# A BF16 product on TensorE in place of VectorE's additions for the band mask of windowed attention, in one hybrid encoder block

## The reference

```python
sc = jnp.einsum('bnqhgd,bnkhd->bnhgqk', qb, kb).astype(jnp.float32) * (ATT_HD ** -0.5)
...
valid = (jnp.abs(qpos[:, :, None] - kpos[:, None, :]) <= WINDOW) \
    & (kpos >= 0)[:, None, :] & (kpos < s)[:, None, :]
sc = jnp.where(valid[None, :, None, None], sc, -jnp.inf)
m = jnp.maximum(jnp.max(sc, axis=-1, keepdims=True), snk)
p = jnp.exp(sc - m)
p = p / (jnp.sum(p, axis=-1, keepdims=True) + jnp.exp(snk - m))
```

## Time and profile before

| | |
|---|---|
| median of 3 runs | 1995.5 us (1993.83 to 1995.56) |
| the profiled execution, its own time | 1994.98 us |
| its span | 1993.2 us |
| PE busy | 98% of the span |
| DVE busy | 67% |
| ACT busy | 40% |
| mean granted TensorE clock | 0.995 of full speed |
| attention stage (1016 to 1182 us) | 166 us |

### The profile page before, as it was taken

One profiled execution on the slowest core, in us unless ns is written; L12 is line 12 of the kernel. 1 busy time (PEld: TensorE's weight loads), 2 busy tenths in 40 slices (PEclk: granted clock), 3 DMA queues, 4 the chain that ended last, 5 costly groups with the idle time before them and its releaser, 6 DMA issues. The chain is left out here.

```text
span 1993.2 us, 25435 instructions
## 1 busy us (share of the span) xinstructions
PE 1958.0 (98%) x8988; PEld 1600.0 (80%) x8988; DVE 1338.9 (67%) x1646; ACT 802.8 (40%) x1066; POOL 851.3 (43%) x569
## 2 busy tenths in 40 slices
PE   7999999999999999999999999999999999999997
PEld 5888888888888778888876678888888888878886
DVE  7866666677676855466876665457866666677666
ACT  6433333345554432222135453335333333355542
POOL 0344444368776222422222212242434334577782
PEclk9999999999999999999999999999999999999998
DMA  3333232356353142412111134341433332474532
GB/s 136 114 118 108 89 116 97 135 200 233 127 164 117 63 148 91 179 43 65 42 64 43 64 107 137 128 156 53 137 100 109 106 100 91 146 267 150 197 104 85
DMA packets 110331, 235.74 MB, mean 118 GB/s; under 512 B 9648, under 2 KB 30256, under 8 KB 110256
## 3 DMA queue, kind: packets, MB, share of 16 engines
q1 hardware_dynamic: 79424, 186.15, 27.5%
q10 hardware_dynamic: 30832, 48.60, 7.1%
HBM read 169.18 MB, written 65.54 MB: 118 GB/s over the span
## 5 line engine op out<-in xcount | busy, mean ns | idle before, releaser
L1881 DVE SCALAR_TENSOR_TENSOR x<-ps,x 128x512 f32<-128x512 f32 x280 | 189.4, 688 | 116.8 <-PE ps L781 114.3
L2437 POOL TENSOR_TENSOR gb<-gb,rstd 128x512 f32<-128x512 f32 x42 | 92.4, 2199 | 309.1 <-DVE gb L1807 289.8
L2422 POOL TENSOR_TENSOR w_lo<-stage,w_hi 128x1024 fp32r<-128x1024 f32 x38 | 95.3, 2509 | 286.2 <-ACT w_hi L1158 286.2
L724 PE MATMUL ps<-a_hi,w_hi 128*128 128x512 f32 x528 | 180.0, 402 | 0.6 <-DVE a_lo L2365 0.5
L724 PE MATMUL ps<-a_hi,w_lo 128*128 128x512 f32 x528 | 173.4, 390 | 0.0
L724 PE MATMUL ps<-a_lo,w_hi 128*128 128x512 f32 x528 | 173.4, 390 | 0.0
L781 PE MATMUL ps<-t_hi,hi_a 128*128 128x512 f32 x392 | 153.5, 391 | 1.6 <-DVE t_lo L1777 1.6
L781 PE MATMUL ps<-t_hi,hi_b 128*128 128x512 f32 x392 | 153.2, 391 | 1.6 <-DVE g_of L2111 1.5
L781 PE MATMUL ps<-a_hi,hi_a 128*128 128x512 f32 x384 | 150.2, 391 | 3.6 <-DVE lo_a L1782 3.6
L781 PE MATMUL ps<-t_hi,lo_a 128*128 128x512 f32 x392 | 153.3, 391 | 0.0
L781 PE MATMUL ps<-t_lo,hi_a 128*128 128x512 f32 x392 | 153.1, 391 | 0.0
(11 more groups left out here) (330 smaller groups left out, 4756.2 us busy)
## 6 DMA issues: line engine op xcount, KB each, us to landing
st_a<-win SPq DMA_DIRECT2D x49, 512.0 KB, 3.4
st_b<-win SPq DMA_DIRECT2D x49, 512.0 KB, 4.2
stage<-wstream SPq DMA_DIRECT2D x42, 512.0 KB, 3.5
b_spill<-diff SPq DMA_DIRECT2D x82, 256.0 KB, 3.7
t_lo<-b_spill SPq DMA_DIRECT2D x40, 512.0 KB, 7.1
b_spill<-rawv SPq DMA_DIRECT2D x66, 256.0 KB, 4.1
a_lo<-b_spill SPq DMA_DIRECT2D x30, 512.0 KB, 4.6
x<-xT SPq DMA_DIRECT2D x16, 512.0 KB, 6.5
```

The lines of the kernel that those rows point to most:

```text
L724: mm = pe.matmul(ps[:, bank, :], w[0:r, k, :], mv[0:r, k, HALF * half:HALF * half + HALF], start=first and part == 0, stop=final and part ...
L1881: dve.scalar_tensor_tensor(out=x[:, m, part], in0=ps[:, bank, :], scalar=0.5, in1=x[:, m, part], op0=ALU.mult, op1=ALU.add).then_inc(xacc, 1)
L2422: pool.tensor_tensor(w_lo[:, parity, :, :], stage[:, parity, :, :], f32(w_hi[:, parity, :, :]), ALU.subtract).then_inc(wlo_done, 1)
L2437: pool.tensor_tensor(gb[:, R], gb[:, R], rstd[:, R], ALU.mult).then_inc(g2_scaled, 1)
```

## The change

PE adds the band: after the four score products of a set it multiplies the BF16 identity (stationary) with the band's block of 128 keys (moving) and accumulates the product onto the scores in PSUM, one product for each head and side. DVE's additions and their semaphore `banded` are gone, so the maximum waits for the scores' semaphore alone, which the last band product now raises. ACT makes the BF16 identity from the FP32 one, behind the DMA of the band, and PE, not DVE, waits for the band ahead of block 0.

```diff
--- before.py
+++ after.py
@@ -235,6 +235,7 @@
         bands = at("bands", [P, 2, CH * P], BF16, offset=AT_BLO + 15 * KB)
         qs = at("qs", [P, QA, P], F32, offset=AT_BLO + 19 * KB)
         vs = at("vs", [P, 2, 3, 64], F32, offset=AT_BLO + 21 * KB)
+        ident16 = at("ident16", [P, P], BF16, offset=AT_BLO + 30 * KB)
         p0 = at("p0", [P, GRP, 3 * P], F32, offset=AT_P0)
         p1 = at("p1", [P, GRP, 3 * P], F32, offset=AT_BLO + 24 * KB)
         pr = (p0, p1)
@@ -307,7 +308,7 @@
         va_turned, va_nat = sem("va_turned"), sem("va_nat")
         qs_done, vs_done = sem("qs_done"), sem("vs_done")
         half_done, half_evac = sem("half_done"), sem("half_evac")
-        s_done, banded, max_done = sem("s_done"), sem("banded"), sem("max_done")
+        s_done, ident_done, max_done = sem("s_done"), sem("ident_done"), sem("max_done")
         m_done, bias_done = sem("m_done"), sem("bias_done")
         exp_done, den_done, rden_done, p_done = sem("exp_done"), sem("den_done"), sem("rden_done"), sem("p_done")
         p_turned, pT_done, pv_done, yatt_done = sem("p_turned"), sem("pT_done"), sem("pv_done"), sem("yatt_done")
@@ -1031,8 +1032,13 @@
                 lo, hi = key_span(i)
                 for a in range(GRP):
                     rows = slice(64 * (a % 2), 64 * (a % 2) + 64)
-                    mm = pe.matmul(ps[:, 2 + a, lo:hi], qs[rows, 2 * kv + a // 2, :], km[kv][rows, i * P + lo:i * P + hi],
-                                   start=True, stop=True)
+                    pe.matmul(ps[:, 2 + a, lo:hi], qs[rows, 2 * kv + a // 2, :], km[kv][rows, i * P + lo:i * P + hi],
+                              start=True, stop=False)
+                for a in range(GRP):
+                    sides = [side for side in range(2) if 2 * side in key_blocks(i)]
+                    for side in sides:
+                        mm = pe.matmul(ps[:, 2 + a, 2 * side * P:2 * side * P + P], ident16[:, :],
+                                       bands[:, side, i * P:i * P + P], start=False, stop=side == sides[-1])
                 mm.then_inc(s_done, 1)
 
             def turn_p(i, kv, pos):
@@ -1093,6 +1099,8 @@
 
             pe.wait_ge(kmask_done, 4)
             pe.wait_ge(evac, U_GATE - 1)
+            pe.wait_ge(bands_loaded, 16)
+            pe.wait_ge(ident_done, 1)
             attention_block(0, U_GATE, U_GATE % 2, None)
             attention_block(1, U_GATE + 1, (U_GATE + 1) % 2, 0)
             for i in range(2, CH):
@@ -1603,6 +1611,7 @@
                 if j == QA + 2:
                     act.wait_ge(yret_done, RH)
                     act.dma_start(bands[:, :, :], band).then_inc(bands_loaded, 16)
+                    act.activation(ident16[:, :], ident, ACT.Copy).then_inc(ident_done, 1)
                 split(U_ATT + j, (U_ATT + j) % 2)
 
 
@@ -2295,14 +2304,8 @@
 
             def maxima(i, kv, at):
                 c0 = 2 * i + kv
-                sides = [side for side in range(2) if 2 * side in key_blocks(at)]
                 lo, hi = key_span(at)
                 dve.wait_ge(s_done, c0 + (1 + SEED))
-                for side in sides:
-                    s = ps[:, 2:6, 2 * side * P:2 * side * P + P]
-                    dve.tensor_tensor(s, s, bands[:, side:side + 1, bass.ds(i * P, P)].to_broadcast([P, GRP, P]),
-                                      ALU.add).then_inc(banded, 3 - len(sides))
-                dve.wait_ge(banded, 2 * c0 + 2)
                 dve.tensor_reduce(mx[:, :], ps[:, 2:6, lo:hi], AX.X, ALU.max).then_inc(max_done, 1)
                 dve.wait_ge(max_done, c0 + 1)
 
@@ -2344,7 +2347,6 @@
                 dve.wait_ge(unit_done, n + 1)
                 dve.tensor_tensor(raw[:, HALF:TOK], ps[:, 1, :], rstd[:, HALF:TOK], ALU.mult).then_inc(evac, 1)
 
-            dve.wait_ge(bands_loaded, 16)
             for b in range(2):
                 attention_block(b, U_GATE + b, b, 16 * SEED, b)
             with dve.Fori(1, CH // 2 - 1) as it:
```

## The result

The changed kernel takes 2000.08 us (median of 7 runs, 1997.15 to 2003.56) against 1994.73 us before in the same sessions (7 runs, 1993.83 to 1999.75): a ratio of 1.0024 with a 95% interval of 1.0014 to 1.0034, so slower by 2.8 to 6.8 us. The profiled execution took 2000.08 us with a span of 1998.2 us at a granted clock of 0.996.

What follows compares the result with a forecast made beforehand. PE was taken to bound the attention stage, with DVE covered. Products 7.3 us, less 0.4 hidden in block 0 and 0 from DVE's relief, gave 6.9 us over 1995.5: 2002.4 us, range 2000.3 to 2008.0.

Steps and rivals of the forecast that it cites:

- The bound: Attention stage: PE's work is the time (busy 164.4 of 166 us), DVE's is covered; relieving DVE gains 0.
- The count, the place, the moved waits: Attention stage: 112 new PE records; identity copy, band DMA and POOL's qs cost nothing; DVE busy 19 us less.
- The price of a product: Each band product: 53.8 ns streaming plus 11.6 fixed, 65.4 ns; 7.3 us in all, bounds 6.0 to 13.7.
- The switch: From 64-row scores to full-array work, 0.20 us a group: met by the new products, no second one; bound 3.2 us.
- Rival C: Around each score group: products fill the idle 0.20 us, 3.2 of 7.3 us free; 1999.2 us, not slower; chance 0.06.
- Block 0: First attention block: PE's waits for kc (0.17 us) and p (0.44 us) swallow 0.4 us of the new products.
- The sum: Whole kernel: 7.3 - 0.4 - 0 = 6.9 us, added to the median of 1995.5, gives 2002.4 us.
- Rivals A and B: Band products' loads set the pace, 109 ns (2007.1 us, chance 0.22), or hide half, 87 ns (2004.7 us, chance 0.14).
- D: Band products cost more: a second switch per group (2005.6 us) or two records each (2009.6 us); chance 0.06.
- The range: Whole kernel's time: 2000.3 to 2008.0 us, including the run-to-run spread of 1.7 us.

Runs made afterwards that it cites:

- the extra FP32 records: Changed kernel plus 64 FP32 products of 128 columns, eight in each attention block's second half pass, into an unused bank: 2013.75 us (one run).
- the FP32R group: Changed kernel plus 64 FP32R products of 128 columns, eight in each attention block's second half pass, into an unused bank: 2008.29 us (one run).

## Why the prediction was right in direction and wrong in size

- **The bound.** Right. PE is the stage's time before and after, and DVE's relief is worth nothing: the kernel without any band has the same stage to 0.03 us.
- **The count, the place, the moved waits.** Right. 112 records, one each; copy of the identity, the DMA of the band and POOL's qs nowhere in PE's waits. The wait for p fell to 0.26 us ("about 0.2"). DVE is busy 17.6 us less, not 19: 28 x 692 ns adds up records that overlap, and their busy time in the earlier trace rows is 18.3 us. Its idle time ahead of the maximum did not grow "by as much": 3.8 us there, the rest ahead of rden, gs and sg.
- **The price of a product: the first of two terms that failed.** The 7.3 us of the sum are 112 products of 65.4 ns, made of 53.8 for streaming and 11.6 as "the fixed part of a record"; this choice among the three values was the author's estimate. The steps are 57.3 ns. The 11.6 ns came from what 512-column FP32R products take over their columns, and do not stand behind each 128-column BF16 product: there some 2.5 ns do, and 10 ns more behind the first of a group. 104 exposed products x 8.1 ns = 0.84 us too much.
- **The switch: the second, as large.** "The switch is met by them, not by what follows. I count no second one": right that there is no second one, but the term for what the switch hides was put at nothing. The sum had only the 0.20 us up to the gate product's start. The gate product behind the scores then also took 0.34 us instead of 0.227, and in this slow start lies the last product of each group: 0.41 us for eight, not 0.46. Over 14 groups of 57 ns 0.8 us. Rival C had something hidden, in the wrong place and size: nothing fills the 0.20 us, which are paid as before. The load of the first full-array product starts 0.41 us behind the start of the last score record in both kernels (1087.18 behind 1086.77 before, 1037.21 behind 1036.80 after).
- **Block 0.** "Total 0.4 us" of 0.5 was to be hidden; all of it is, 0.02 us are left of eight products. 0.1 us.
- **The sum.** 12 groups of 0.41 to 0.43 us, 0.17 and 0.19 us in block 7 and 0.02 in block 0 make 5.3 us, where 6.9 was forecast; the parts above are 0.84 + 0.8 + 0.1 = 1.7 for a gap of 1.6. The other 0.7 us between 2002.4 and 2000.1 is the base: three runs had a median of 1995.5, seven have 1994.7.
- **Rivals A and B**, 0.36 of the chance, fell: BF16 loads stay hidden behind 57 ns steps, with records of 98 ns, each from the third of a group on starting 2 ns behind the start of the product ahead. Their rows were of another type, as the text said against them. D fell too: one record each, no second switch. The waits of PE that DVE or ACT could end add up to 1.1 us in the earlier trace rows, not 1.2; nothing hangs on it.
- **The range.** It reached 5.6 us above the forecast and 2.1 below, though the text's own lower bound of 6.0 us for the term gives 1995.5 + 6.0 - 0.4 = 2001.1 us, and with the base's spread of 1.7 us 1999.4.
- **Right for a wrong reason.** "A score group of 8 records takes 1.49 us with 384 columns and 1.06 with 256: 53.8 ns for 128 columns" took the records to run one behind the other. They run two at a time, each at twice that: a pair takes 0.32 us for 384 columns, 107 ns per 128, as the FP32 transposes do at 109 and the extra FP32 records at 112. So 109 ns, the whole ground of rival A, also fits FP32's own streaming, and tells nothing of a BF16 load.

Rows on the load: BF16 steps of 57 ns with a 98 ns load record stand beside some 112 ns with 192 ns records in FP32R and FP32. In the kernel before, the load of a 512-column gate product, 188 ns long, starts 3 ns behind the start of the product ahead and 0.22 us before its own product (846.86 for the one at 847.08), so it lies beneath the product ahead. The loads of the eight FP32 transposes have records of 138 to 142 ns and start 107 to 110 ns apart, from 847.54 on each 1 to 2 ns behind the start of the product ahead. So these rows alone cannot tell a load that sets the pace from one that follows it; that a load can set it the FP32R group shows (below), and that it does not in BF16 the 57 ns show.

## What to carry to other kernels

Work moved from a covered engine to the engine that bounds a stage costs its price there, less what an existing wait or slow start hides (one product in eight here, and block 0), and the price of a small matmul is read from starts of the same type: here 57 ns for 128 BF16 columns with a load of their own, half of FP32R or FP32. Put such products behind a whole group of half-array products, not between them: grouped they cost 5.3 us in this stage, interleaved 38. Before a duration is divided by its records, look at single starts, since records may run side by side.

## What the runs showed of the hardware beyond what was expected

- FP32R, which takes 227 ns for 512 columns, is no faster than an FP32 record for 128: of a group of eight the first step is 57 or 58 ns, the other six are 109 to 115. The first product is the one whose load ran beneath the 512-column product ahead; its record is 220 ns long, like the BF16 ones, the others some 274, and their loads start 108 to 112 ns apart. So the load sets the 112, and the 128 columns alone take 58. An FP32 record takes 109 ns from the first step on, behind the same hidden load, so there the columns alone take about as long as the load.
- 64-row FP32 products that follow each other run two records at a time: in the kernel before the two start 6 to 7 ns apart, and one pair 0.32 us behind another with 384 columns. With full-array products between them four heads take 4 x 0.84 us, and 1.49 us together. The pairs remain with neighbours on the same half of the array (groups of 1.50 us against 1.49). Which records pair there no run shows, and it stays open.
- The stage's length repeats: 160.92, 160.95, 160.94 and 161.04 us in four kernels whose stage came out the same, while the time of one kernel varies by 7 us from run to run. A change of one stage is judged on the stage first.
